# Opening of a fused two-block kernel: activation load issued behind the second modulation slab, mixer constants issued at the opening's end

## The reference

```
c_act = silu(c)
mod = c_act @ w_ada + b_ada                       # (1024) @ (1024, 9216): nine vectors of 1024
sh1, sc1, g1, sh2, sc2, g2, sh3, sc3, g3 = split(mod, 9)
u = rmsnorm(x, norm_ffn1) * (1 + sc1) + sh1
h = x + 0.5 * g1 * swiglu(u, w_ffn1_up, w_ffn1_down)
u = rmsnorm(h, norm_mix) * (1 + sc2) + sh2
h = h + g2 * hybrid_mixer(u, ...)                 # convolutions, gated delta rule, gates
u = rmsnorm(h, norm_ffn2) * (1 + sc3) + sh3
h = h + 0.5 * g3 * swiglu(u, w_ffn2_up, w_ffn2_down)
```

## Time and profile before

| | |
|---|---|
| median of 3 runs | 1773.03 us (1771.96 to 1773.1) |
| the profiled execution, its own time | 1772.8 us |
| its span, first to last instruction | 1771.0 us |
| PE busy | 1603.3 us, 91% of the span |
| DVE busy | 1035.6 us, 58% |
| ACT busy | 750.1 us, 42% |
| mean granted TensorE clock | 0.943 |
| read from HBM | 251.87 MB |

### The profile page before, as it was taken

One profiled execution on the slowest core, in us unless ns is written; L12 is line 12 of the kernel. 1 busy time (PEld: TensorE's weight loads), 2 busy tenths in 40 slices (PEclk: granted clock), 3 DMA queues, 4 the chain that ended last, 5 costly groups with the idle time before them and its releaser, 6 DMA issues. The chain is left out here.

```text
span 1771.0 us, 33806 instructions
## 1 busy us (share of the span) xinstructions
PE 1603.3 (91%) x14218; PEld 1539.5 (87%) x14218; DVE 1035.6 (58%) x1589; ACT 750.1 (42%) x1029; POOL 61.8 (3%) x82
## 2 busy tenths in 40 slices
PE   2999989989998889999799997899998888899997
PEld 2999979989997879999688986899997776789997
DVE  6999466887645666444586524544336556365443
ACT  2554344872215444443460103466333345456432
POOL 0121000001100001110000000000000000000000
PEclk7999999999999999999899987999999988799998
DMA  9899535432113537555331002254542321235451
GB/s 355 305 340 344 196 129 206 157 132 91 62 49 113 191 135 249 185 179 182 105 119 32 2 2 72 83 179 144 189 167 81 121 93 48 72 118 179 161 184 48
DMA packets 39195, 256.78 MB, mean 145 GB/s; under 512 B 4259, under 2 KB 5668, under 8 KB 9892
## 3 DMA queue, kind: packets, MB, share of 16 engines
q1 hardware_dynamic: 37492, 251.07, 40.3%
q10 hardware_dynamic: 1584, 3.97, 0.6%
HBM read 251.87 MB, written 3.15 MB: 144 GB/s over the span
## 5 line engine op out<-in xcount | busy, mean ns | idle before, releaser
L456 DVE TENSOR_TENSOR w_lo<-raw,w_hi 128x2048 fp32r<-128x2048 f32 (+2 forms) x203 | 456.6, 2249 | 461.2 <-ACT w_hi L448 460.3
L530 PE MATMUL bank<-x_hi,w_hi 128*128 128x256 f32 (+1 forms) x1840 | 535.3, 291 | 46.3 <-DVE x_lo L679 27.3
L448 ACT ACTIVATE w_hi<-raw 128x2048 fp32r<-128x2048 f32 (+2 forms) x203 | 381.4, 1879 | 394.3 <-PE bank L532 364.6
L531 PE MATMUL bank<-x_lo,w_hi 128*128 128x256 f32 (+1 forms) x1840 | 527.7, 287 | 0.0
L532 PE MATMUL bank<-x_hi,w_lo 128*128 128x256 f32 (+1 forms) x1840 | 526.8, 286 | 0.0
L530 PEld LDWEIGHTS bank<-x_hi,w_hi 128*128 128x128 f32 x1840 | 353.0, 192 | 54.4 <-issue 44.6
L532 PEld LDWEIGHTS bank<-x_hi,w_lo 128*128 128x128 f32 x1840 | 354.1, 192 | 0.0
L531 PEld LDWEIGHTS bank<-x_lo,w_hi 128*128 128x128 f32 x1840 | 352.5, 192 | 0.9 <-issue 0.7
L530 PE MATMUL bank<-mh_hi,w_hi 128*128 128x272 f32 (+1 forms) x512 | 148.3, 290 | 6.5 <-PEq L2668 6.5
L532 PE MATMUL bank<-mh_hi,w_lo 128*128 128x272 f32 (+1 forms) x512 | 147.1, 287 | 0.0
L531 PE MATMUL bank<-mh_lo,w_hi 128*128 128x272 f32 (+1 forms) x512 | 146.4, 286 | 0.0
(11 more groups left out here) (504 smaller groups left out, 2562.6 us busy)
## 6 DMA issues: line engine op xcount, KB each, us to landing
raw<-in_stream SPq DMA_DIRECT2D x227, 1024.0 KB, 4.8
raw<-in_stream SPq DMA_DIRECT2D x8, 768.0 KB, 4.3
gate_store<-stage ACTq DMA_DIRECT2D x8, 256.0 KB, 2.1
raw<-in_stream SPq DMA_DIRECT2D x4, 512.0 KB, 3.6
h<-in_h ACTq DMA_DIRECT2D x1, 1088.0 KB, 5.6
zt<-gate_store SPq DMA_DIRECT2D x1, 1024.0 KB, 6.1
gate<-gate_store SPq DMA_DIRECT2D x1, 1024.0 KB, 8.2
out<-h SPq DMA_DIRECT2D x8, 128.0 KB, 1.9
```

The source lines that it names most:

```text
L448: nc.scalar.activation(w_hi[:, s_at % 2, 0:kt], raw[:, r_at % RING, 0:kt], ACT.Copy).then_inc(hi_done, 1)
L456: nc.vector.tensor_tensor(w_lo[:, s_at % 2, 0:kt], raw[:, r_at % RING, 0:kt], w_hi[:, s_at % 2, 0:kt].bitcast(F32), ALU.subtract).then_inc ...
L530: nc.tensor.matmul(out, hi, xh[:, k0 + k, 0:L], start=start, stop=False)
L531: nc.tensor.matmul(out, hi, xl[:, k0 + k, 0:L], start=False, stop=False)
```

## The change

ACT no longer issues `h` and the rest of `cst` at its start. The issue of `h` stands behind Silu and behind a wait for the full landing of ring place 1, that is of slab 1. The issue of the rest of `cst` stands at the end of ACT's list of the opening, behind `split_hi` of slab 8, and ACT doesn't wait for it. The wait for it is now the first instruction of SP in the first swiglu's block, ahead of the load of slab 13. The second swiglu gets no such wait.

```diff
@@ opening, L712
             def _(act):
                 act.dma_start(cst[:, 0:NEEDED], t["const"][:, 0:NEEDED]).then_inc(need_in, 16)
-                act.dma_start(h[:], t["h0"]).then_inc(h_in, 16)
-                act.dma_start(cst[:, NEEDED:const_cols], t["const"][:, NEEDED:const_cols]).then_inc(rest_in, 16)
                 act.wait_ge(vec_in, 16)
                 nc.scalar.activation(c_act[:], col("c", 0, 8), ACT.Silu).then_inc(c_ready, 1)
+                act.wait_ge(raw_full[1], LANDED)
+                act.dma_start(h[:], t["h0"]).then_inc(h_in, 16)
                 act.wait_ge(h_in, 16)
                 for u in range(4):
                     norm_ffn1.square(act, u, sq0)
                 norm_ffn1.root_on_act(act)
                 split_hi(act, (S["up1"], 0, numbers(S["up1"], None, 0, 0, 0)))
-                act.wait_ge(rest_in, 16)
+                act.dma_start(cst[:, NEEDED:const_cols], t["const"][:, NEEDED:const_cols]).then_inc(rest_in, 16)
@@ swiglu, L1036
-        def swiglu(ups, down, gate, norm, then):
+        def swiglu(ups, down, gate, norm, then, late=None):
...
                     def _(sp):
+                        if late:
+                            late(sp)
                         load_to(sp, down.r0 + 12 + RING)
@@ L1128
-        swiglu([S["up1"]], S["down1"], 2, norm_ffn1, norm_mix)
+        swiglu([S["up1"]], S["down1"], 2, norm_ffn1, norm_mix, lambda sp: sp.wait_ge(rest_in, 16))
```

## The result

| | before | after |
|---|---|---|
| median, 8 runs each | 1773.36 us | 1779.80 us |
| ratio (95% interval) | | 1.0036 (1.0021 to 1.0051) |
| profiled execution, its own time | 1772.8 us | 1778.95 us |
| its span | 1771.0 us | 1777.1 us |
| mean granted clock of TensorE | 0.943 | 0.944 |

What follows compares the result with a forecast made beforehand. PE was taken to be busy for 91% of the span, with DVE's list setting the opening's end. The terms -3.8 + 1.9 + 2.9 gave +1.0 to 1.1 us, a median of 1774.1 us, range 1771.0 to 1777.0.

Steps and rivals of the forecast that it cites:

- What bounds the kernel: Whole kernel: PE is busy for 91% of the span; DVE's list sets the opening's end.
- the carry one for one: From 60 us on PE has no idle time, so the opening's gain or loss reaches the end unchanged.
- Step 1: Opening: slab 0 lands at 6.5 us and slab 1 at 9.0, so DVE starts 3.8 us earlier.
- Step 2: Opening: h, issued at 9.05 us, takes 7.6 us (5.6 to 9.3) and lands at 16.65.
- The turns: While h moves, both queues alternate packet by packet; its 128 rows cost 128 slab packets, 2.5 us more.
- rival A: Opening: h goes ahead of the slabs and lands at 14.65; -0.8 us, 1772.2 us; chance 0.23.
- Step 3: Root of the norm: waits 2.9 us for PE's sums, starts at 22.85 against 21.71, 1.1 us later.
- Steps 4 to 6: Behind the root: later slabs, moved constants and SP's new wait cost nothing; bounds 1 us or below.
- B: Opening: h lines up behind queued slabs, landing at 18.35; +2.8 us, +4.2 with PE slow throughout; chance 0.22.
- The scatter: Total time: half a us of chance variation, included in the range.
- 8.8 us of slack: Opening: PE's sums of squares end at 12.92 us and DVE reads them at 21.71; the change spends this.

Runs made afterwards that it cites:

- e6: Kernel before plus nine idle DVE instructions (3.9 us in all) ahead of the root, nothing else changed; ratio to the kernel before 1.0017 (1.0000 to 1.0033).
- Experiments 4 and 5: e4 and e5: the changed kernel with h issued without the wait for slab 1, ratio 1.0018; and with h issued into an empty SP queue, ratio 1.0009.
- e9: The kernel before against itself, no edit, for a second profile; ratio 0.9994 (0.9966 to 1.0023), span 1776.2 us.
- e2: The changed kernel with h issued at ACT's start as before, so only the constants are late; ratio to the kernel before 1.0003 (0.9976 to 1.0030).
- e3: The changed kernel with h issued on SP's own queue between slabs 1 and 2; ratio to the kernel before 0.9985 (0.9970 to 1.0000), median 1772.97 us.
- e5: The changed kernel with SP issuing slabs 2 and later only once ACT has issued h; ratio to the kernel before 1.0009 (0.9991 to 1.0027).
- e4: The changed kernel without the wait for slab 1, h issued right behind Silu; ratio to the kernel before 1.0018 (0.9987 to 1.0049).
- e8: The changed kernel with ACT waiting for slab 0 in place of slab 1 before issuing h; ratio to the kernel before 1.0015 (0.9997 to 1.0033).
- e11: The changed kernel with the constants at ACT's start as before, so only h is late; ratio to the kernel before 1.0009 (0.9983 to 1.0036).
- e12: Second timing of e3's version, h on SP's queue behind slab 1 and constants late; ratio to the kernel before 0.9990 (0.9979 to 1.0001).
- e7: The changed kernel with h on SP's queue behind slab 3, root behind slab 5, first pair's sums ahead of the squares; ratio to the kernel before 0.9988.
- e10: The changed kernel again, a third time, no edit; ratio to the kernel before 1.0027 (1.0015 to 1.0039), span 1781.2 us.
- experiment 2: The run e9, the kernel before against itself without an edit; ratio 0.9994 (0.9966 to 1.0023).

## Why the prediction was wrong

*What bounds the kernel, and the carry one for one:* nothing speaks against it. In e6 an opening later by 3.3 us made the kernel 3.0 us slower, though the interval (0.0 to 5.9) is too wide to show one for one.

*Step 1:* right where slab 0 behaved. It landed 4.9 us after its issue, DVE started at 6.74. I hadn't seen that it can take 5.9 to 7.2 us with nothing large ahead of it, which moved h's issue to 10.1 and 11.4 in the other two executions. That is another 1 us on average.

*Step 2 failed.* I put h's issue to landing at 7.6 us and 9.3 as the upper end. It was 9.4, 9.5 and 8.8. The turns were right: from its first packet at 12.6 h needs 5.9 us, and 7.6 less the 1.6 us that the kernel before has from h's issue to its first packet is 6.0. What was missing is the wait before the first packet, 3.5 us in place of those 1.6. The row for it was there: from 3.2 to 5.0 us one queue had 98.7% of the time with two slabs issued on the other. I read it as a question of who goes first and gave it to rival A in h's favour. It is a question of who is issued beside a queue that already holds work, and in the changed kernel that is h. Experiments 4 and 5 show this: with the queue full the lag is 3.5 us at another place in the stream too, with the queue empty h needs 5.1 us in all.

The Trainium skill, in DMA: Bandwidth & Descriptors, section Queues, rings and completion order, has each DMA engine go round between the queues that have work, packet by packet. The stretch from 13 to 17 us agrees (109 packets against 110), the one from 9.2 to 12.4, with none of h, doesn't.

*Step 3:* the new wait stood where I said, but the sum came out otherwise. I had -3.8 for the start of DVE, +1.9 of wait for slab 3 and +2.9 for the sums. Measured are -3.6, +0.2 and +7.0, together 3.6 of the 3.7 us. The wait for slab 3 stayed out because h moved nothing in front of it, so all the lateness fell on the sums. Landing to root took 6.8 us and not 6.2: the sums ran 5.93 us. Stretches of L630 alone, against the earlier trace rows:

```profile
19.41:24.00 4.59, 4.59 (x11) 3.69 (x12) 1.00 1.01 421
24.00:25.34 1.34, 1.34 (x7) 0.84 (x5) 1.00 1.00 416
```

PE stayed at the slow pace (0.42 us each) for 4.6 us and not for 3.3 before it rose. That isn't the change's doing: in e9 the kernel before has 6.27 us, so my 5.33 was one of several values. With 1.8 us more from h's issue to landing, the issue itself 0.1 later and the sums 0.6 longer, 22.85 becomes 25.35; measured is 25.39.

*Steps 4 to 6:* right for the opening. From the root to the first x_hi nothing is added, neither by the constants' move nor by SP's wait, and the moved constants alone bring 1.3 us (e2). The 1.1 us of the first swiglu stay without a cause.

*The rivals:* B had the price (h lands 9.3 us after its issue, +2.8 to +4.2), and half of its mechanism: h does wait for slabs queued before it, but for at most about 180 packets of them (experiments 4 and 5). It had 0.22 where it should have had most. A loss of more than 3.5 us had 0.07, and the first timing shows 6.4.

*The scatter:* I took half a us from three runs. Two profiles of the kernel before lie 5.2 us apart with the same opening, so a median of 1779.8 is the 3.7 to 4.9 us of the opening plus what chance adds or takes. Six of the first eight times of the kernel before lie at 1772.0 to 1773.6; in the three later timings its medians were 1775.2 to 1777.3, for nearly half of its executions had a mean clock of 0.940 or less and took 1778 to 1779. The low median of the kernel before in the first timing was in part luck. Why just that timing came out at 6.4 us isn't settled further.

## What to carry to other kernels

A DMA that is to arrive at a given place in a saturated stream belongs on the queue of that stream: there its place is kept (h landed at 11.8 in e3), while on another queue it first waited for what the stream's queue held, up to 3.5 us, and then shared half and half (18.6 in the changed kernel). Before work is taken from the front of a queue, add up what the moved transfer itself releases (here 6.8 us from h to the root) and compare that with the slack; 8.8 us of slack were spent on 11.8 us of delay. A gain of a few us in a kernel of 1.8 ms has to be read in the opening's timeline; the total can move by 5 us by itself.

## What the runs showed of the hardware that was not expected

- **The lag of a queue that starts beside a busy one.** It goes with what the other queue holds at the issue: 1.0 us from issue to first packet with nothing held (e5), 2.2 to 2.8 with 108 to 114 packets, most of a slab (the late constants), and 2.0 to 3.5 with 134 to 499 packets held (h in the changed kernel, e4, e8 and e11). In e5 it struck the slabs (issued at 9.78, first packet at 13.3), in the changed kernel h.
- **The first slab's time to landing.** Issued at 1.65 out of the loop over the ring, with only the small loads ahead: 4.9, 5.9, 7.2, 6.4 and 7.2 us (the changed kernel three times, e4, e8). In the four executions whose first slabs are issued one by one, from 1.51 on (e3, e12, e5, e7): 5.0, 4.8, 5.0 and 5.0. A few of the engines are late, not all: when slab 0 landed at 8.8 in e10, SP's queue had moved 2.21 MB, nearly a slab more than slab 0 and the small vectors (1.25 MB). Why, no run tells.
- **TensorE's granted clock in the opening.** The rows print 1.00 for the sums from the start, but the pace is that of 1.2 GHz (0.42 us each, then 0.22) for the first 8 to 13 matmuls, 8 and 12 in two executions of the kernel before. Here the pace tells the level, not the printed share.
- **Where the clock falls later is not the same in two executions of one program** (384 to 412 us in experiment 2), and the span differs with it.
